# One decoder layer on one core: the second tile of 128 tokens is moved from lockstep with the first into the first tile's expert gather

## What is computed

```python
def hybrid_layer(h, mem, ...):
    n = rmsnorm(h, mix_norm_gain)
    proj = n @ w_in
    ...
    y_att = dsa_attention(q, k, v, iq, ik, iw)
    y_rwkv = rwkv7_time_mix(rwkv_p, ...)
    y_mem = memory_cross_attention(memq_p, mem, ...)
    up = jnp.einsum('bscw,cwd->bscd', branches, w_up)
    gates = jax.nn.sigmoid(gate_p.reshape(B, S, N_BRANCH, D) + gate_bias)
    h = h + jnp.sum(gates * up, axis=2) @ w_out
    return h + peer_ffn(rmsnorm(h, ffn_norm_gain), ...)

def one_block(args):          # in peer_ffn; e = 8 heads x 16 experts of a token
    ue, ve = u[et], v[et]
    hid = jax.nn.gelu(jnp.einsum('td,ted->te', xt, ue), approximate=False)
    return jnp.einsum('te,ted->td', gt * hid, ve)
```

## Time and profile before

| | us |
|---|---|
| runs | 1179.42, 1181.05, 1183.85 (median 1181.05) |
| profiled execution | 1186.98, its span 1185.2 |
| TensorE busy | 973.7 of the span |
| VectorE busy | 726.4 |
| ScalarE busy | 238.3 |
| GpSimd busy | 303.4 |
| moved by DMA | 329.59 MB, of it 268.45 MB by the gather |

### The profile page before, as it was taken

One profiled execution on the slowest core, in us unless ns is written; L12 is line 12 of the kernel. 1 busy time (PEld: TensorE's weight loads), 2 busy tenths in 40 slices (PEclk: granted clock), 3 DMA queues, 4 the chain that ended last, 5 costly groups with the idle time before them and its releaser, 6 DMA issues.

```text
span 1185.2 us, 15243 instructions
## 1 busy us (share of the span) xinstructions
PE 973.7 (82%) x5148; PEld 618.5 (52%) x5148; DVE 726.4 (61%) x1812; ACT 238.3 (20%) x587; POOL 303.4 (26%) x293
## 2 busy tenths in 40 slices
PE   6999999999999999998897666866666676678666
PEld 6888888888889978774452222222222222222212
DVE  0452331296537342346677877887688778877885
ACT  2014133214312110222212111111121021101111
POOL 0000000041005100023444333444433444334431
PEclk9997999999999999998999989898977989898989
DMA  7342433312212125576989999999999999999996
GB/s 287 126 159 71 142 107 107 107 63 80 72 36 72 42 105 199 210 309 257 422 356 421 420 422 422 422 422 422 421 363 419 419 421 423 421 422 423 421 422 267
DMA packets 46397, 329.59 MB, mean 278 GB/s; under 512 B 5264, under 2 KB 5648, under 8 KB 6800
## 3 DMA queue, kind: packets, MB, share of 16 engines
q0 software_dynamic: 36864, 268.45, 54.8%
q1 hardware_dynamic: 8928, 58.81, 13.9%
q10 hardware_dynamic: 560, 1.70, 0.4%
HBM read 327.90 MB, written 1.05 MB: 278 GB/s over the span
## 4 chain that ended last, share of the span: by engine, by line
PE 52%; DVE 19%; DMA 16%; issue 10%; ACT 2%; POOL 1%; DVEq 0%; POOLq 0%; ACTq 0%
PE psum_proj L613 19%; DMA pool_mem<-in_experts,pool_mem 15%; PE psum_job L994 8%; PE psum_proj L626 5%; PE psum_proj L994 3%; PE psum_proj L961 3%; DVE pool_mem L1757 3%; DVE pool_mem L1698 2%; DVE pool_mem L522 2%; PE psum_job L854 2%; PE psum_job L874 2%; PE psum_job L864 1%; DVE pool_mem L1695 1%; DVE pool_mem L1735 1%; DVE pool_mem L1702 1%
## 5 line engine op out<-in xcount | busy, mean ns | idle before, releaser
L994 PE MATMUL psum_job<-pool_mem 64*64 64x512 f32 x1536 | 353.5, 672 | 92.4 <-DVE pool_mem L522 92.4
L1828 POOL DMA_INDIRECT pool_mem<-in_experts,pool_mem x256 | 264.4, 1033 | 505.4 <-PE psum_job L994 255.1
L1757 DVE CUSTOM_DVE_ANT_0 pool_mem<-pool_mem 128x1024 f32<-128x1024 f32 x256 | 312.9, 1222 | 106.9 <-DMA pool_mem<-in_experts,pool_mem 105.3
L613 PE MATMUL psum_proj<-pool_mem 128*128 128x256 f32 x1152 | 261.9, 387 | 11.9 <-DVE pool_mem L1315 9.3
L994 PEld LDWEIGHTS psum_job<-pool_mem 64*64 64x64 f32 x1536 | 112.3, 148 | 287.8 <-issue 286.5
L613 PEld LDWEIGHTS psum_proj<-pool_mem 128*128 128x128 f32 x1152 | 220.9, 194 | 48.5 <-issue 9.3
L994 PE MATMUL psum_proj<-pool_mem 64*64 64x512 f32 x512 | 147.9, 703 | 85.0 <-DVE pool_mem L522 85.0
L1253 ACT ACTIVATE pool_mem<-pool_mem 128x1 f32<-128x1 f32 x256 | 51.2, 202 | 487.3 <-DVE pool_mem L1757 486.8
L994 PEld LDWEIGHTS psum_proj<-pool_mem 64*64 64x64 f32 x512 | 40.9, 151 | 171.5 <-issue 170.5
L1810 POOL TENSOR_TENSOR pool_mem<-pool_mem,const 128x512 f32<-128x512 f32 x24 | 31.5, 1333 | 355.2 <-DVE pool_mem L1559 295.8
L522 DVE TENSOR_SCALAR pool_mem<-const,pool_mem 128x64 f32<-128x64 f32 x256 | 79.9, 312 | 33.7 <-ACT pool_mem L1253 31.7
(11 more groups left out here) (258 smaller groups left out, 876.5 us busy)
## 6 DMA issues: line engine op xcount, KB each, us to landing
pool_mem<-in_weights SPq DMA_DIRECT2D x51, 1024.0 KB, 4.9
pool_mem<-in_experts,pool_mem POOLq DMA_INDIRECT x256, 11.3
pool_mem<-in_xT SPq DMA_DIRECT2D x1, 1024.0 KB, 5.1
pool_mem<-in_memT SPq DMA_DIRECT2D x1, 1024.0 KB, 10.7
pool_mem<-in_x ACTq DMA_DIRECT2D x1, 1024.0 KB, 8.5
out<-pool_mem SPq DMA_DIRECT2D x2, 512.0 KB, 5.7
const<-in_const SPq DMA_DIRECT2D x1, 872.5 KB, 14.4
rows<-in_rows SPq DMA_DIRECT2D x1, 512.0 KB, 16.1
```

Source lines behind the costliest of these rows:

```text
L613: ins = mm(o[:, m, :], lhsT=w[:, k, m * P:(m + 1) * P], rhs=src[:, k, :], start=(k == 0), stop=(k == KT - 1))
L994: ins = mm(sum_bank(t, odd, d)[strip:strip + 64, :], lhsT=diag[rows_, g % DIAGS, :], rhs=slot[g % SLOTS][rows_, D + 512 * d:D + 512 * d + ...
L1757: ins = V.tensor_tensor_reduce(u, u, xn_tok[:, t, :], 1.0, 0.0, ALU.mult, ALU.add, hid[:, par, s_:s_ + 1])
L1828: G_.indirect_dma_start(slot[s_ % SLOTS], None, t_in["experts"], bass.IndirectOffsetOnAxis(ap=expert_i[:, par, s_:s_ + 1], axis=0)).then_i ...
```

## The change

From the gates on, each tile has its own products, 128 columns wide. The order of all engines is one list, `STEPS`, in three parts. `first_tile` takes tile 0 alone through inverse, recurrence, gates, merge and output projection, three of its eight query units, and the choice of head 0; the attention of tile 1 is in it too. `second_tile` is the first tile's gather: a pair of slots (`slots`, p) at a time, and before each pair one step of tile 1's chain (`chain`, 36 of them, from p = 1) and one filling unit (`fill`, 27 of them, from p = 0: the queries and keys of heads 3 to 7 of tile 0, and gates and up units of tile 1). `third_part` is the start of tile 1's gather with the last five queries; the last four heads run in a loop.

The weights of gates, up, output and query units are loaded once for each tile. Adds are made in pairs of slots (`add_pair`), eight matmuls at a time, and both buffers come free at its end. The sums of both tiles use the same four PSUM banks, so the second tile's sums begin after the first tile's are evicted; the other late products share two banks. Attention takes only the keys that a tile can reach (128 for tile 0). Some operations of the front are split by tile for a new memory layout.

```diff
+def first_tile():
+    steps = [("sumsq", "q"), ("gram", 0, 0), ("gate", 0, 2), ("sumsq", "k"), ("gram", 0, 1), ("spread", "q"), ("spread", "k"),
+             ("rope", "q"), ("invA", 0, 0), ("rope", "k"), ("gate", 0, 3), ("top", 0), ("invA", 0, 1), ("gate", 0, 4),
+             ("invX", 0, 1), ("invT", 0, 1), ("gate", 0, 5), ("invA", 0, 2), ("score", 0, 0), ("gate", 0, 6),
+             ("exp", 0, 0), ("invX", 0, 2), ("score", 0, 1), ("invT", 0, 2), ("top", 1), ("gate", 0, 7), ("scale", 0, 0),
+             ("exp", 0, 1), ("turn", 0, 0), ("invA", 0, 3), ("gate", 0, 8), ("scale", 0, 1), ("invX", 0, 3), ("score", 0, 2),
+             ("value", 0, 0), ("turn", 0, 1), ("exp", 0, 2), ("invT", 0, 3), ("gate", 0, 9), ("value", 0, 1), ("score", 0, 3),
+             ("scale", 0, 2), ("exp", 0, 3), ("invA", 0, 4), ("turn", 0, 2), ("gate", 0, 10), ("invX", 0, 4), ("scale", 0, 3),
+             ("value", 0, 2), ("turn", 0, 3), ("invT", 0, 4), ("gate", 0, 11), ("value", 0, 3), ("invA", 0, 5)]
+    steps += [("up", 0, 0), ("up", 0, 1), ("invT", 0, 5), ("up", 0, 2), ("score", 1, 0), ("rhs", 0), ("exp", 1, 0), ("up", 0, 3),
+              ("u", 0), ("score", 1, 1), ("y", 0), ("scale", 1, 0), ("up", 0, 4), ("exp", 1, 1), ("rhs", 1), ("turn", 1, 0),
+              ("u", 1), ("scale", 1, 1), ("score", 1, 2), ("value", 1, 0), ("y", 1), ("up", 0, 5), ("turn", 1, 1), ("exp", 1, 2),
+              ("norm", 0), ("value", 1, 1), ("score", 1, 3), ("scale", 1, 2), ("exp", 1, 3), ("up", 0, 6), ("turn", 1, 2),
+              ("scale", 1, 3), ("up", 0, 7), ("value", 1, 2), ("turn", 1, 3), ("yt", 0), ("value", 1, 3)]
+    steps += [("up", 0, u) for u in range(8, 12)]
+    for i in range(5):
+        steps += ([("out", 0, i)] if i < 4 else []) + ([("ht", 0, i - 1)] if i > 0 else [])
+    steps += [("rstd", 0), ("query", 0, 0), ("keys", 0, 0), ("sums", 0), ("query", 0, 1), ("keys", 0, 1), ("choose", 0),
+              ("xn", 0), ("query", 0, 2), ("keys", 0, 2), ("gate", 1, 0), ("gate", 1, 1), ("gate", 1, 2)]
+    return steps
+def second_tile():
+    chain = [[("gram", 1, 0)], [("gram", 1, 1)], [("invA", 1, 0)]]
+    for l in range(1, LEVELS):
+        chain += [[("invA", 1, l)]] + ([[("invX", 1, l)]] if l < LEVELS - 1 else []) + [[("invT", 1, l)]]
+    for n in (2, 3):
+        chain += [[("rhs", n)], [("u", n)], [("y", n)]]
+    chain += [[("norm", 1)], [("yt", 1)], [("up", 1, 8), ("up", 1, 9)], [("up", 1, 10), ("up", 1, 11)]]
+    for i in range(5):
+        chain.append(([("out", 1, i)] if i < 4 else []) + ([("ht", 1, i - 1)] if i > 0 else []))
+    chain += [[("rstd", 1), ("query", 1, 0)], [("keys", 1, 0), ("query", 1, 1)], [("keys", 1, 1), ("query", 1, 2)],
+              [("keys", 1, 2), ("xn", 1)]]
+    fill = []
+    for u in range(8):
+        fill += [[("up", 1, u)], [("gate", 1, u + 3)]]
+    fill.append([("gate", 1, 11)])
+    for n, h in enumerate(range(3, PEER_HEADS)):
+        fill[4 * n + 1:4 * n + 1] = [[("query", 0, h)], [("keys", 0, h)]]
+    steps = []
+    for p in range(PAIRS):
+        if p > 0 and chain:
+            steps += chain.pop(0)
+        if fill:
+            steps += fill.pop(0)
+        steps.append(("slots", p))
+    assert not chain and not fill
+    return steps
+def third_part():
+    steps = [("flush", 0), ("slots", PAIRS), ("evict", 0), ("sums", 1)]
+    h = 3
+    for p in range(PAIRS + 1, PAIRS + UNROLLED * TOPK // 2):
+        if h < PEER_HEADS and p % 4 == 1:
+            steps.append(("query", 1, h))
+        if h < PEER_HEADS and p % 4 == 2:
+            steps.append(("keys", 1, h))
+            h += 1
+        steps.append(("slots", p))
+    assert h == PEER_HEADS
+    return steps + [("flush", 1)]
+STEPS = first_tile() + second_tile() + third_part()
...
+            def load(n):
+                if n >= RING:
+                    sp.wait_ge(proj_full, LAST_UNIT[n - RING] + 1)
+                sp.dma_start(wring[n % RING].rearrange("p a b -> p (a b)"), t_in["weights"][USES[n]]).then_inc(
+                    weights_in[n % RING], 16)
...
+            for n in range(RING, len(USES)):
+                load(n)
...
+            def begin_sums(t):
+                if t == 0:
+                    for b in range(LATE_BANKS, BANKS):
+                        pe.wait_ge(bank_free[b], EARLY_USES[b])
+                else:
+                    pe.wait_ge(sg["o_sb_ok"], 2 * t)
+                for odd in range(2):
+                    for d in range(2):
+                        ins = mm(sum_bank(odd, d), lhsT=c("zeros") if odd else ident, rhs=h_tok[t][:, 512 * d:512 * d + 512],
+                                 start=True, stop=True, skip_group_check=True)
+                ins.then_inc(sg["sums_begun"], 1)
...
+            def add_pair(j, s):
+                wait_alone(pe, sg["diag_ok"], j + 2)
+                for d in range(2):
+                    for odd in range(2):
+                        for i in range(2):
+                            rows_, strip = slice(64 * i, 64 * i + 64), 64 * (i ^ odd)
+                            ins = mm(sum_bank(odd, d)[strip:strip + 64, :], lhsT=diag[rows_, (s + odd) % DIAGS, :],
+                                     rhs=slot[(s + odd) % SLOTS][rows_, D + 512 * d:D + 512 * d + 512],
+                                     start=False, stop=True, skip_group_check=True)
+                        if d == 1:
+                            ins.then_inc(sg["slot_free"], 1)
+            def slots(p):
+                if p % PAIRS > 0:
+                    add_pair(2 * p - 2, 2 * p - 2)
+            def flush(t):
+                p = PAIRS if t == 0 else FIRST_LOOPED // 2
+                add_pair(2 * p - 2, 2 * p - 2)
...
+            def dot(par, n, s_, t):
+                dve.wait_ge(slot_in[s_ % SLOTS], (n * 2 + s_ // SLOTS) * 16 + 16)
+                u = slot[s_ % SLOTS][:, 0:D]
+                V.tensor_tensor_reduce(u, u, xn_tok[t], 1.0, 0.0, ALU.mult, ALU.add,
+                                       hid[:, par, s_:s_ + 1]).then_inc(sg["dots"], 1)
+            def diagonal(par, s_, done, early=False):
+                dve.wait_ge(sg["gelu_ok"], done)
+                if not early:
+                    dve.wait_ge(sg["slot_free"], done - DIAGS)
+                V.tensor_scalar(diag[:, s_ % DIAGS, :], c("two_idents"), act_h[:, par, s_:s_ + 1],
+                                gate_e[:, par, s_:s_ + 1], ALU.mult, ALU.mult).then_inc(sg["diag_ok"], 1)
+            def last_diagonal(j):
+                diagonal(j // TOPK % 2, j % TOPK, j + 1, j < DIAGS)
+            def slots(p):
+                for j in (2 * p, 2 * p + 1):
+                    n, s_ = j // TOPK, j % TOPK
+                    if j % TILE_SLOTS == 0:
+                        dve.wait_ge(sg["xn_ok"], j // TILE_SLOTS + 1)
+                    if s_ == 0:
+                        dve.wait_ge(sg["gate_ok"], n + 1)
+                    dot(n % 2, n, s_, j // TILE_SLOTS)
+                    if j % TILE_SLOTS > 0:
+                        last_diagonal(j - 1)
+                    if s_ in PARTS:
+                        PARTS[s_](1 - n % 2, n + 1)
...
+            def gather(j):
+                n, s_ = j // TOPK, j % TOPK
+                if s_ == 0 or j % TILE_SLOTS == 0:
+                    pool.wait_ge(sg["experts_ok"], n + 1)
+                if j == 6:
+                    pool.wait_ge(sg["sums_begun"], 1)
+                    pool.wait_ge(sg["xn_ok"], 1)
+                if j >= SLOTS:
+                    pool.wait_ge(sg["slot_free"], j - SLOTS + 1)
+                G_.indirect_dma_start(slot[s_ % SLOTS], None, t_in["experts"],
+                                      bass.IndirectOffsetOnAxis(ap=expert_i[:, n % 2, s_:s_ + 1], axis=0)
+                                      ).then_inc(slot_in[s_ % SLOTS], 16)
+            def choose(n):
+                for j in range(SLOTS):
+                    gather(j)
+            def slots(p):
+                if p % PAIRS > 0:
+                    for j in (2 * p + SLOTS - 2, 2 * p + SLOTS - 1):
+                        if j < FIRST_LOOPED:
+                            gather(j)
...
+            def gate(t, i):
+                wait_unit(act, ("gate", t, i))
+                if t == 1 and i >= GATE_RING:
+                    wait_unit_read(act, ("up", t, i - GATE_RING))
...
-            def add_group(t, n, g):
-                wait_alone(pe, sg["diag_ok"], n * HEAD_GROUPS + (g + 1))
-                odd = g % 2
-                for d in range(2):
-                    for i in range(2):
-                        rows_, strip = slice(64 * i, 64 * i + 64), 64 * (i ^ odd)
-                        ins = mm(sum_bank(t, odd, d)[strip:strip + 64, :], lhsT=diag[rows_, g % DIAGS, :],
-                                 rhs=slot[g % SLOTS][rows_, D + 512 * d:D + 512 * d + 512],
-                                 start=False, stop=True, skip_group_check=True)
-                ins.then_inc(sg["group_free"], 1)
```

1388 lines of the change are left out of this document (663 added, 725 removed).

## The result

The changed kernel takes 1214.82 us (median of four, 1209.48 to 1216.88), the kernel before 1182.45 in the same comparison: 1.0265 times as long, 95% interval 1.0218 to 1.0312. The prediction was 1196. The direction held. The time lies above the likeliest case's own range (1180 to 1212) and inside the wide one (1148 to 1230); the rise that was forecast, 1.3%, is half of the 2.7% that came.

The account below looks back on a forecast made before the run. The prediction saw a TensorE-bound stage followed by a DMA-bound gather. Terms A to H, from start to end, summed to a span of 1199.9 us; plus 1.8 less 5.9 gave 1196 us, range 1148 to 1230.

Parts of the forecast that it names:

- the likeliest case: The forecast itself: interleaved cycles average 8.4 us, whole kernel 1196 us, own range 1180 to 1212; chance 0.42.
- D: First query to first pair of adds: TensorE's work about 30 us, then VectorE's 11; adds at 424.5.
- F: Rest of tile 0, without chain or fill: 28 cycles of 4.97 us, DMA bound, 139 us.
- E: Interleaved part, 35 cycles between adds: TensorE and VectorE wait on each other, 269 us plus 25, 294 us.
- A: Start to the schedule: two gate units made for one tile bring its start from 219.6 to 212.8 us.
- B: Schedule's start to its first gate: 23.7 us less 3.4 for a halved gate unit, reaching 233.1.
- C: First tile up to its first query: 122 us of TensorE's work plus 27 of stalls, query at 382 to 383.
- G: Tile 1's gather: 128 slots at 2.49 us (318), five query blocks 12.4, boundary 5.6; ends at 1193.7.
- the lump of 25: Added to E's cycles: non-dense adds 9, GpSimd's masks and sums 6, DMA-last stretches 6, lower TensorE clock 4.
- rival 4: Ring by pairs runs dry in F and G, 0.2 us in each of 91 pairs: 18 us more, 1214; chance 0.12.
- Rival 2: Engines slide past each other in E, DMA stays full: E 241, total 1143, or 1165 halfway; chance 0.28.
- Rivals 3 and 5: ScalarE's table loads and port lock exposed in E, 1228; or GpSimd's waiting masks hold gathers, as in 3; together 0.18.

Follow-up runs that it names:

- slots ahead: Changed kernel, but VectorE and ScalarE do a pair's dots, gelus and diagonals before reading that pair's chain step and filling unit: 1202.48 us against 1213.96.
- single adds: Adds one slot at a time: changed kernel from pair 37, 1210.37 us; from pair 49, on spread order, slots ahead, moved gates and shorter written-out part, 1176.53 us.
- the blocks cut: 30 second-tile weight blocks loaded only in 128 of 2048 columns: 1207.32 us on the changed kernel, 1169.73 us with slots ahead; second tile's values not the reference's.
- without the tables: Changed kernel with gates 3 to 11 of the second tile through gelu instead of sigmoid, sparing ScalarE's table loads: 1213.44 us against 1213.96.
- the masks twice: Changed kernel with GpSimd making each of the second tile's twelve level masks twice: 1212.80 us against 1213.96.
- the spread order: Changed kernel with the second tile's chain steps and filling units spread over pairs 1 to 60, not 1 to 36: 1213.68 us; with slots ahead 1178.79 us.

## Why the prediction had the direction right and the size wrong

The mechanism of the interleaved part was right. What failed are other terms of the sum: the step from span to median (-4.1 us; +8.0 and +4.0 measured), D (41.5; 48.7 and 51.2) and F (139.0; 147.2 and 145.1). Together they were 24 to 28 us short, and E gave back 6 to 12 of it. The prediction's own terms, in us of the span, against two profiled executions of the changed kernel. The ends are those of its text: the schedule's first product (L678), the start of gate 3, the first query, the first pair of adds, the adds of pair 36, the end of the last adds of tile 0, the end of the last adds, the span.

| term | predicted | first profile | second profile |
|---|---|---|---|
| A to the schedule | 212.8 | 205.0 | 215.4 |
| B to gate 3 | 20.3 | 20.3 | 20.2 |
| C to the first query | 149.9 | 154.9 | 152.2 |
| D to the first adds | 41.5 | 48.7 | 51.2 |
| E interleaved | 294.0 | 287.6 | 282.0 |
| F rest of tile 0 | 139.0 | 147.2 | 145.1 |
| G tile 1 | 336.2 | 337.0 | 337.7 |
| H end | 6.2 | 6.2 | 6.2 |
| span | 1199.9 | 1206.8 | 1210.0 |
| span to median | -4.1 | +8.0 | +4.0 |

**E was right in its mechanism, and it was what decided.** Cycles of 8.2 and 8.1 us on average (8.4 predicted), DMA at 0.85 to 0.86, and the pace that of a lockstep, as the pair of runs with slots ahead showed (38 us once DMA is out of the way). That the size came out so near is in part luck: the cycles that the walk had at 53, 59, 70, 59 and 28, 269 in all, measure 62, 67, 71, 62 and 25 in the first profile, 288 in all, so the walk was 19 short (13 in the second), mostly in the first fifteen cycles, and the lump of 25 on top covered it. That the gain of 100 us before the gather would be given back came out, down to the place: slot 72 is reached at 715.2 before and 714.7 in the first profile.

**The last step, from span to median, was mis-sized by 12 us against the first profile, where it is the largest term, and by 8 against the second.** The prediction took 5.9 off, because the one profiled execution of the kernel before lay 5.9 over its median. Executions of one kernel differ more than that. The profiled execution of the kernel before had TensorE at the lower clock for some 14 us near 105 us (below), and so has the second profile here; the first has not. With it, the profiled executions of eight kernels of this family came out at -5.2 to +9.0 us from their kernel's median, +1.4 on average; without it, five came out at -10.4 to -5.2. An offset of one execution was carried over to another kernel, and A, taken from the same execution, with it: hence 205.0 or 215.4 for the 212.8.

**D was 7 to 10 short.** The rows of the second profile, from the first query to the first adds:

```profile
387.82 3.81 PE L637 MATMUL psum_proj<-pool_mem 128*128 128x128 f32 x32 [1.02 <-ACT pool_mem L1237]
415.11 3.84 PE L637 MATMUL psum_proj<-pool_mem 128*128 128x128 f32 x32 [1.23 <-DMA pool_mem<-in_weights]
421.14 2.05 PE L984 MATMUL psum_proj<-pool_mem 128*128 128x128 f32 x16 [2.19 <-DMA pool_mem<-in_weights]
430.78 2.67 PE L863 MATMUL psum_job<-pool_mem 64*128 64x256 f32 x8 [6.52 <-DVE pool_mem L1584]
433.38 5.68 PE L637 MATMUL psum_proj<-pool_mem 128*128 128x128 f32 x32
438.99 1.95 PE L1034 MATMUL psum_job<-pool_mem 64*64 64x512 f32 x16
```

The walk put 30 us of TensorE's work there and let VectorE's chain of 11 end last. It left out that `gram`'s second half waits for VectorE's mask of the first (6.5, behind the choice of a head), that blocks for gate and up come late (1.2 and 2.2) and that the products after that wait run at the lower clock (granted 0.50 from 431.0 to 433.4 us): the query takes 5.7 instead of 3.7.

**F was 6 to 8 short, and G's sum came out by luck.** F's 28 cycles end with the start of the last adds; up to there it is 144.0 and 143.2 us, 5.0 and 4.2 more than the 139. The last adds themselves take 3.2 and 1.9, and the prediction has them nowhere. Of the 5.0 and 4.2, 2.3 are the weight block that moves 0.92 MB (0.96) inside F; some 0.1 us a pair is left. G counts five query blocks, 12.4 us, where two come (5.0). What made up for the missing 7.4 is a longer boundary and dearer slots: slots 192 to 240, without a weight block, take 124.5 and 122.4 us, before 119.3, or 0.2 and 0.1 us more a pair. That is up to rival 4's size, in G as in F, but its cause, the adds by pairs, is not shown: single adds left the rest of tile 0 as it was and gave 4 us in tile 1 in one pair of runs, 1 in the other. GB/s in 40 slices, the changed kernel from 716 to 860 us, and the kernel before from 720 to 860:

```profile
GB/s 423 419 426 412 416 426 423 421 423 398 405 360 350 362 373 423 421 428 428 421 421 423 419 419 360 416 428 414 426 428 414 426 398 355 410 416 348 403 423 430
```

```profile
GB/s 419 428 419 424 421 426 414 426 426 419 419 421 426 419 424 419 428 417 424 421 424 419 424 421 421 426 417 426 419 424 417 426 424 414 419 431 424 414 424 426
```

The rate is the same, but for dips to 350 to 375 in the changed kernel. The prediction's case against rival 4 was that three slots stay in flight. It did not see that TensorE would run at 0.72 of its clock there; but with the clock back at 0.92 the stretch took as long. What brings the dips stays open; the choice of a head, which the prediction named, the lower clock and the fetching of instructions were not tried apart.

**C was 2 to 5 short,** not by its stalls but by its work: TensorE is idle for 24.7 us in both profiles (27 predicted) and busy for 130.2 and 127.5 (122), at a granted clock of 0.93 and 0.96. Two of the places were right: 6.9 us before the turn of head pair 0, and 7.2 behind the norm.

**Rival 2** (DMA stays full, 1143) did not come: the order of the readers and the order of the steps both stand against it. The nearest that was reached with all the weights is 1176.5. With the blocks cut it is 1169.7, although DMA needs only 70 x 2.49 = 174 us for E then: the stretch still takes 246.5, with TensorE busy for 232.8 of 270 us. So a third limit, TensorE's own work and waits, lies close to DMA's 241, and the walk of rival 2 had it at 225. **Rivals 3 and 5** are out: without the tables, and with the masks twice, the time is the same within the intervals. In sum: E came out shorter than predicted, C, D, F and G longer, and the step to the median went the other way; that is how 1.3% became 2.7%.

One reading of the trace before does not hold as it stands, without weight in the sum: the dot does not wait for its DMA in every slot, but 25 times from 720 to 840 us, in 48 slots.

## What to carry to other kernels

Where two engines hand work to each other in a fixed cycle, ask of each engine's order what stands ahead of the operation that the other waits for. Put the short operations that feed the next adds ahead of the reading of what is being made; but price it together with the resource that is next late, since here slots ahead alone gave 11.5 us, the spread order alone nothing, and both together 35. An offset between one profiled execution and a median belongs to that execution: go from the predicted span by the spread of several, not by one difference.
